# Head pairs in two halves of the array, or queries padded with zeros to all 128 rows

## The reference

```python
def forgetting_attention(q, k, v, log_f):          # A: 16 heads, causal, blocks of 128 queries
    c = jnp.cumsum(log_f, axis=1).transpose(0, 2, 1)
    for i in range(S // Q_BLOCK):
        s = einsum("bqhd,bkhd->bhqk", q[:, q0:q1], k[:, :q1]) * scale
        s = s + c[:, :, q0:q1, None] - c[:, :, None, :q1]
        p = softmax(where(causal, s, -inf))
        outs.append(einsum("bhqk,bkhd->bqhd", p, v[:, :q1]))

def dilated_branch(q, k, v, dil, slopes):          # B: 3 groups of 8 heads, dil = 1, 4, 16
    s = einsum("bnirhd,bnjrhd->bnrhij", qb, kk) * Dh ** -0.5
    s = where(valid, s - slopes * dil * dist, -inf)
    p = exp(s - max(s)); l = sum(p)                # o = (p / l) v, lse = max + log(l)
    # block: alpha = softmax of lse over the 3 groups, o = sum(alpha * o_g)
```

## Time and profile before

| | us |
|---|---|
| median of 3 runs (lowest, highest) | 2764.49 (2764.15, 2768.72) |
| profiled execution | 2764.49 |
| its span | 2762.7 |
| PE busy | 2673.2 (97%) |
| DVE busy | 1395.0 (50%) |
| ACT busy | 983.4 (36%) |
| POOL busy | 89.6 (3%) |

### The profile page before, as it was taken

One profiled execution on the slowest core, in us unless ns is written; L12 is line 12 of the kernel. 1 busy time (PEld: TensorE's weight loads), 2 busy tenths in 40 slices (PEclk: granted clock), 3 DMA queues, 4 the chain that ended last, 5 costly groups with the idle time before them and its releaser, 6 DMA issues.

```text
span 2762.7 us, 30936 instructions
## 1 busy us (share of the span) xinstructions
PE 2673.2 (97%) x12410; PEld 2151.1 (78%) x12410; DVE 1395.0 (50%) x2249; ACT 983.4 (36%) x1555; POOL 89.6 (3%) x99
## 2 busy tenths in 40 slices
PE   7999999999998699999998899999999999999999
PEld 6866888888787578888874588888888678888887
DVE  4455674664433667457557544434453155544342
ACT  3255442343225654234433432223312242422231
POOL 2000000000000000000010000000020220000000
PEclk9999999999999899999999899999999999999999
DMA  4300233233221022322321023322333022233222
GB/s 143 101 30 32 85 99 99 92 99 107 92 99 64 12 76 92 107 85 98 113 99 39 12 91 97 99 91 92 101 98 129 24 77 92 96 103 99 92 92 92
DMA packets 65520, 237.55 MB, mean 86 GB/s; under 512 B 7409, under 2 KB 7537, under 8 KB 65249
## 3 DMA queue, kind: packets, MB, share of 16 engines
q1 hardware_dynamic: 63648, 229.38, 25.6%
q0 software_dynamic: 1728, 6.19, 0.7%
HBM read 233.45 MB, written 2.10 MB: 85 GB/s over the span
## 4 chain that ended last, share of the span: by engine, by line
PE 90%; DVE 5%; ACT 4%; issue 1%; DMA 0%; SPq 0%; DVEq 0%; ACTq 0%
PE ps L420 28%; PE ps L422 28%; PE ps L421 28%; PE ps L525 2%; PE ps L799 1%; PE ps L561 1%; PE ps L542 1%; ACT m_A_P L1642 1%; ACT m_B_P L1642 1%; DVE m_B_P L948 1%; PE ps L786 1%; DVE m_A_st L952 1%; PE ps L497 0%; PE ps L483 0%; ACT m_E_P L1642 0%
## 5 line engine op out<-in xcount | busy, mean ns | idle before, releaser
L420 PE MATMUL ps<-m_xs,m_wsp 128*128 128x512 f32 x2232 | 880.6, 395 | 20.1 <-DVE m_xs L848 10.8
L422 PE MATMUL ps<-m_xs,m_wsp 128*128 128x512 f32 x2232 | 872.2, 391 | 0.0
L421 PE MATMUL ps<-m_xs,m_wsp 128*128 128x512 f32 x2232 | 871.8, 391 | 0.0
L1540 ACT ACTIVATE m_wsp<-m_raw 128x1024 fp32r<-128x1024 f32 x429 | 446.8, 1053 | 796.9 <-PE ps L422 761.9
L837 DVE TENSOR_TENSOR m_wsp<-m_raw,m_wsp 128x1024 fp32r<-128x1024 f32 x429 | 519.3, 1225 | 207.1 <-ACT m_wsp L1540 206.8
L420 PEld LDWEIGHTS ps<-m_xs,m_wsp 128*128 128x128 f32 x2232 | 421.5, 189 | 114.9 <-issue 18.4
L421 PEld LDWEIGHTS ps<-m_xs,m_wsp 128*128 128x128 f32 x2232 | 421.7, 189 | 89.3 <-issue 2.9
L422 PEld LDWEIGHTS ps<-m_xs,m_wsp 128*128 128x128 f32 x2232 | 421.0, 189 | 88.4
L887 DVE TENSOR_TENSOR m_x<-m_x,ps 128x512 f32<-128x512 f32 x104 | 70.8, 687 | 313.2 <-PE ps L422 313.2
L420 PE MATMUL ps<-m_wsp,m_xs 128*128 128x512 f32 x320 | 125.2, 391 | 0.0
L422 PE MATMUL ps<-m_wsp,m_xs 128*128 128x512 f32 x320 | 125.0, 391 | 0.0
(11 more groups left out here) (313 smaller groups left out, 3275.7 us busy)
## 6 DMA issues: line engine op xcount, KB each, us to landing
m_raw<-in_w SPq DMA_DIRECT2D x429, 512.0 KB, 3.3
m_x<-in_xT SPq DMA_DIRECT2D x4, 512.0 KB, 9.2
m_B_bias<-in_biasB POOLq DMA_DIRECT2D x8, 256.0 KB, 3.1
out<-m_x SPq DMA_DIRECT2D x8, 256.0 KB, 2.0
m_O_D<-in_decay POOLq DMA_DIRECT2D x1, 1024.0 KB, 5.1
m_A_sel<-in_sel POOLq DMA_DIRECT2D x1, 512.0 KB, 3.5
m_E_sel<-in_sel POOLq DMA_DIRECT2D x1, 512.0 KB, 3.5
m_O_cs<-in_ropeo POOLq DMA_DIRECT2D x1, 512.0 KB, 3.7
```

The lines of the kernel that those rows point to most:

```text
L420: e.matmul(out, lh, rh, start=first, stop=False)
L421: e.matmul(out, lh, rl, start=False, stop=False)
L422: return e.matmul(out, ll, rh, start=False, stop=final)
L1540: e.activation(wsp[n % NSP][:, 0, :], raw[n % NRAW][:, :], ACT.Copy).then_inc(*s_hi(n))
```

## The change

The queries of a head are copied by POOL into a tile of 128 partitions whose other half is zero (`A_qz`, two buffers for each parity; `B_qz`, one for each parity), with a new function `pad` and a new semaphore. A score matmul then multiplies this padded tile with all 128 partitions of `A_k` or `B_k`: the other head's keys meet zeros. Scores are issued job by job. `B_q` and `B_k` are stored in token order; in groups 1 and 2 the matmul itself reads every fourth column of both operands. In DVE's attention `among(i)` is moved ahead of `normalized(i-1)`. Two small tiles (`line`, `O_rc`) change place or size.

```diff
@@ tiles
-        line = sb(ctx, "line", [128, 24])
+        line = sb(ctx, "line", [128, 8])
+            A_qz = [ring(c, f"A_qz{p}", 2, [128, S]) for p in range(2)]
+                B_qz = [ring(c2, f"B_qz{p}", 1, [128, S]) for p in range(2)]
-            O_rc = sqs[1][:, 0:32].rearrange("p (h c) -> p h c", h=4)
+            O_rc = sb(c, "O_rc", [128, 4, 8])
@@ -511,27 +513,21 @@
                 P, PT = spec["P"], spec["PT"]
                 def scores(u):
-
                     for j in u.jobs:
                         b = take("score", pre, "score", j.n)
                         q.wait_ge(*free[b])
-                        free[b] = s_top[pre, j.n] if pre == "B" else s_exp[pre, j.n]
                         for w in spec["ready"](u, j):
                             q.wait_ge(*w)
-                    for si in range(len(u.jobs[0].segs)):
-                        last = {}
-                        for j in u.jobs:
-                            s = j.segs[si]
-                            last[j] = e.matmul(bank(pre, "score", j.n)[:, s["c0"]:s["c0"] + s["n"]], spec["q"](u, j, s),
-                                               spec["k"](u, j, s), start=True, stop=not spec["more"](j, s))
-                        for j in u.jobs:
-                            s = j.segs[si]
+                        for si, s in enumerate(j.segs):
+                            out = ps[b]
                             more = spec["more"](j, s)
+                            i = e.matmul(out[:, s["c0"]:s["c0"] + s["n"]], spec["q"](u, j, s), spec["k"](u, j, s),
+                                         start=True, stop=not more)
                             for ei, (o, n, lt, rh) in enumerate(more):
-                                last[j] = e.matmul(bank(pre, "score", j.n)[:, s["c0"] + o:s["c0"] + o + n], lt, rh,
-                                                   start=False, stop=ei == len(more) - 1)
-                            if s is j.segs[-1]:
-                                last[j].then_inc(*s_score((pre, j.n)))
+                                i = e.matmul(out[:, s["c0"] + o:s["c0"] + o + n], lt, rh, start=False,
+                                             stop=ei == len(more) - 1)
+                        i.then_inc(*s_score((pre, j.n)))
+                        free[b] = s_top[pre, j.n] if pre == "B" else s_exp[pre, j.n]
                 def turn(u):
                     for j in u.jobs:
@@ -586,13 +582,13 @@
             project_rows(ST["av"], xhalf, lambda k: s_xlo["mix0", k], lambda ci, tb: s_aev["av", ci, tb])
             def A_ready(u, j):
-                return [s_ev["ain", u.p], s_ev["ain", 8 + u.p], s_step["forget", "c"], d_sel["sel"], d_idb["idb"],
+                return [s_pad["A", u.p, j.par], s_ev["ain", 8 + u.p], s_step["forget", "c"], d_sel["sel"], d_idb["idb"],
                         d_mk["mk"], d_id["id"]]
             attention("A", A_units, dict(
                 P=A_P, PT=A_PT, before=nothing, among=nothing, ready=A_ready, vready=s_aev["av", 1, 3],
-                q=lambda u, j, s: A_q[64 * j.par:64 * j.par + 64, u.p, 128 * s["qb"]:128 * s["qb"] + 128],
-                k=lambda u, j, s: A_k[64 * j.par:64 * j.par + 64, u.p, 0:s["n"]],
+                q=lambda u, j, s: A_qz[j.par][u.p % 2][:, 128 * s["qb"]:128 * s["qb"] + 128],
+                k=lambda u, j, s: A_k[:, u.p, 0:s["n"]],
                 more=lambda j, s: [(s["n"] - 128, 128, identb[:, :], maskb[:, 0, :]),
                                    (0, s["n"], A_sel[:, j.h, :], A_c3[:, 0:s["n"]])],
                 v=lambda u, j, kb: A_v[:, kb, 64 * j.h:64 * j.h + 64],
@@ -624,6 +620,9 @@
             def B_tile(u):
                 return 4 * u.g + u.p
+            def B_tokens(u, s):
+                return slice(128 * s["qb"], 128 * s["qb"] + 128) if u.g == 0 else slice(s["qb"], S, 4)
             def B_stats(p, kind):
@@ -683,9 +682,10 @@
             attention("B", B_units, dict(
                 P=B_P, PT=B_PT, before=nothing, among=B_among, vready=s_aev["bv", 2, 3],
-                ready=lambda u, j: [s_ev["bq", B_tile(u)], s_ev["bk", B_tile(u)]],
-                q=lambda u, j, s: B_q[64 * j.par:64 * j.par + 64, B_tile(u), 128 * s["qb"]:128 * s["qb"] + 128],
-                k=lambda u, j, s: B_k[64 * j.par:64 * j.par + 64, B_tile(u), 128 * s["kbs"][0]:128 * s["kbs"][-1] + 128],
+                ready=lambda u, j: [s_pad["B", u.p, u.g, j.par], s_ev["bk", B_tile(u)]],
+                q=lambda u, j, s: B_qz[j.par][0][:, B_tokens(u, s)],
+                k=lambda u, j, s: B_k[:, B_tile(u), 128 * s["kbs"][0]:128 * s["kbs"][-1] + 128] if u.g == 0
+                else B_k[:, B_tile(u), s["qb"]:S:4],
                 more=lambda j, s: [],
                 v=lambda u, j, kb: B_v[:, kb, 512 * u.g + 64 * j.h:512 * u.g + 64 * j.h + 64],
                 evacuated=lambda u: s_ohi["B", B_tile(u)]))
@@ -983,9 +983,9 @@
                         spec["before"](units[i])
                         tops(units[i])
                         negated(units[i])
+                    spec["among"](i)
                     if 1 <= i <= n:
                         normalized(units[i - 1])
-                    spec["among"](i)
                     if i >= 3 and units[i - 3].final:
                         spec["out"](units[i - 3])
@@ -1151,18 +1151,12 @@
-            def by_fourth(m, t):
-                return t[:, :] if m < 4 else t[:, :].rearrange("p (i r) -> p r i", r=4)
...
-                    e.scalar_tensor_tensor(out=as_stored(m, B_q), in0=by_fourth(m, bank("bq", m)), scalar=0.125,
-                                           in1=by_fourth(m, rb("mix1")), op0=ALU.mult, op1=ALU.mult).then_inc(*s_ev(("bq", m)))
+                    e.scalar_tensor_tensor(out=B_q[:, m, :], in0=bank("bq", m)[:, :], scalar=0.125, in1=rb("mix1")[:, :],
+                                           op0=ALU.mult, op1=ALU.mult).then_inc(*s_ev(("bq", m)))
...
@@ -1978,6 +1970,22 @@
             e.memset(A_c3[:, :], 0.0)
             e.memset(A_onr[:, :], 1.0).then_inc(*s_zero("A"))
+            def pad(pre, key, par, dest, src, ready):
+                q.wait_ge(*ready)
+                own = slice(64 * par, 64 * par + 64)
+                e.tensor_copy(dest[own, :], src[own, :]).then_inc(*s_pad((pre, *key, par)))
+            q.wait_ge(*s_zero["A"])
+            for par in range(2):
+                for i in range(2):
+                    e.memset(A_qz[par][i][64 * (1 - par):64 * (1 - par) + 64, :], 0.0).then_inc(*s_zero(("A", par, i)))
+            for p in range(8):
+                for par in range(2):
+                    if p >= 2:
+                        q.wait_ge(*s_score["A", A_units[3 * (p - 2) + 2].jobs[-1].n])
+                    pad("A", (p,), par, A_qz[par][p % 2], A_q[:, p, :], s_ev["ain", p])
             def margins(n, after):
                 q.wait_ge(*after)
@@ -1988,18 +1996,27 @@
             margins(0, s_mm["aout", 7])
             q.wait_ge(*s_mm["f0.dn1", 7])
             e.memset(B_stat[:, :, :, :, :], 0.0).then_inc(*s_zero("B"))
+            q.wait_ge(*s_zero["B"])
+            for par in range(2):
+                e.memset(B_qz[par][0][64 * (1 - par):64 * (1 - par) + 64, :], 0.0).then_inc(*s_zero(("B", par)))
             for u in B_units:
                 if u.n == 4:
                     q.wait_ge(*s_mm["bv", 2, 3])
                     for half in range(2):
                         load(B_selp[half][:, :, :].bitcast(U16), a["selp"][:, 6 * half:6 * half + 6, :], d_selp[half], "selp")
+                    q.wait_ge(*s_pad["B", 0, 2, 1])
                     e.memset(B_pc[:, :, :], 0.0).then_inc(*s_zero("B2"))
                     q.wait_ge(*s_zero["B2"])
-                if u.first and u.g < 2:
-                    a0, a1 = (0, 256) if u.g == 0 else (256, 512)
-                    if u.p:
-                        q.wait_ge(*s_top["B", B_units[u.n - (3 if u.g == 0 else 2)].jobs[-1].n])
-                    load(B_bias[:, :, a0:a1], a["biasB"][:, 2 * u.p:2 * u.p + 2, a0:a1], d_bias[u.g], ("bias", u.p))
+                if u.first:
+                    for par in range(2):
+                        if u.n:
+                            q.wait_ge(*s_score["B", B_units[u.n - 1].jobs[-1].n])
+                        pad("B", (u.p, u.g), par, B_qz[par][0], B_q[:, 4 * u.g + u.p, :], s_ev["bq", 4 * u.g + u.p])
+                    if u.g < 2:
+                        a0, a1 = (0, 256) if u.g == 0 else (256, 512)
+                        if u.p:
+                            q.wait_ge(*s_top["B", B_units[u.n - (3 if u.g == 0 else 2)].jobs[-1].n])
+                        load(B_bias[:, :, a0:a1], a["biasB"][:, 2 * u.p:2 * u.p + 2, a0:a1], d_bias[u.g], ("bias", u.p))
             margins(1, s_mm["bout", 7])
             q.wait_ge(*s_mm["f1.dn1", 7])
             load(E_sel[:, :, :].bitcast(U16), a["sel"], d_selE, "sel")
```

8 lines of the change are left out of this document (2 added, 6 removed).

## The result

The kernel after takes 2786.16 us (median of 4 runs, 2782.41 to 2789.69), the kernel before 2765.34 beside it: a ratio of 1.0074, 95% interval 1.0055 to 1.0091. It is slower by 20.8 us, where 17.2 were forecast (9.2 in A and 8 in B), and the time lies inside the range. The working behind the number did not hold: one term was far too large, and a cause that had been set to zero carries most of the loss.

The account below looks back on a forecast made before the run. TensorE was taken to bound stage A, and a loop of scores, DVE's maxima and ACT's exponentials stage B. 2764.49 + 9.2 (A) + 8 (B) = 2782 us, range 2768 to 2802.

Parts of the forecast that it names:

- Scores in A: Stage A: padded heads run one after the other, costing TensorE more; +9.2 us, between +7.5 and +11.0.
- Stride in B: Stage B, groups 1 and 2: slow strided weight loads set 0.23 us a pass, 3.7 us a unit.
- first rival: Stage B scores: load and stream slowed in turn, 0.46 us a pass, +30 us, 2812 us; chance 0.15.
- the second (free): Rival, stage B scores: the stride costs nothing, B -4 us, 2770 us in sum; chance 0.25.
- B as a whole: Stage B: 5.3 us over three pair periods and 2.5 for the first, +8 us, between -4 and +38.
- +2.5 us for the first pair: Stage B, first pair: copies and strided scores come in a row, +2.5 us once, from 0 to 5.
- the order's -0.8: Stage B, DVE: mixing ahead of the normalization reaches TensorE's transposes 0.8 us earlier, once a pair.
- the zero for group 0: Stage B, group 0: contiguous scores, first head's maxima beside the second's scores; zero, give or take 0.3 us.
- POOL's copies: Two padding copies take 2.1 us, hidden in A and covered in B, the bias load behind them with little room.
- Evacuations of B without the stride: Before stage B: query and key evacuations lose their stride, zero gain since the projection hides them.
- The two moved tiles issue nothing: Tiles `line` and `O_rc`: they issue no instructions, and no cost was counted for moving them.
- third rival: Stage B: strides free and TensorE's clock above 0.95, 10.6 us shorter, 2757 us; chance 0.05.

Follow-up runs that it names:

- jobwise: Kernel before with the scores of A, B and E issued head by head, queries still in halves, no padding; 2784.88 us, ratio 1.0058.
- kcontig: Kernel after with `line` at 24 columns, `O_rc` back in scratch, B's k for groups 1 and 2 stored by fourths, q still strided; 2771.36 us, ratio 1.0023 to before.
- qcontig: Kernel after with `line` at 24 columns, `O_rc` back in scratch, B's q for groups 1 and 2 stored by fourths, k still strided; 2770.33 us, ratio 1.0021 to before.
- contig: Kernel after with `line` at 24 columns, `O_rc` back in scratch, B's q and k stored by fourths and read contiguously; 2767.47 us, ratio 1.0001 to before.
- wgap: Kernel before with weights `wsp` moved 128 bytes, `line` at 16 columns, activation tiles moved 256, 128, 512 and 384 bytes; 2817.48 us, ratio 1.0185.
- ejob: Kernel before with the scores of stage E alone issued head by head; 2762.29 us, ratio 0.9986.
- fact64: Kernel before with a 64-byte gap ahead of the activation tile in each of the four feed-forward blocks; 2773.63 us, ratio 1.0028.

## Why the prediction was right in its number and wrong in its working

**Scores in A: +9.2 us forecast, +0.1 to +1.4 measured.** This step failed, by its own criterion (a pair under 11.6 us). The new price of the groups was right, to 0.1 us. What failed is the sentence that the end of the stage gets all that TensorE gets. One pair of before, timeline of TensorE: the pieces between the scores.

```profile
202.05 0.88 PE L542 MATMUL ps<-m_ident,m_A_P 128*128 128x128 f32 x6
...
204.71 1.16 PE L561 MATMUL ps<-m_A_PT,m_A_v 128*64 128x128 f32 x12
205.80 0.88 PE L542 MATMUL ps<-m_ident,m_A_P 128*128 128x128 f32 x6
...
208.22 1.25 PE L561 MATMUL ps<-m_A_PT,m_A_v 128*64 128x128 f32 x12 [0.16 <-ACT m_A_PT L1651]
209.41 1.09 PE L542 MATMUL ps<-m_ident,m_A_P 128*128 128x128 f32 x8
```

and of after:

```profile
224.11 0.88 PE L538 MATMUL ps<-m_ident,m_A_P 128*128 128x128 f32 x6
224.82 0.39 PE L524 MATMUL ps<-m_A_k,m_A_qz 128*128 128x128 f32 x2
...
226.89 0.88 PE L557 MATMUL ps<-m_A_PT,m_A_v 128*64 128x128 f32 x12
227.69 0.88 PE L538 MATMUL ps<-m_ident,m_A_P 128*128 128x128 f32 x6
...
230.23 0.97 PE L557 MATMUL ps<-m_A_PT,m_A_v 128*64 128x128 f32 x12
231.13 1.09 PE L538 MATMUL ps<-m_ident,m_A_P 128*128 128x128 f32 x8
```

The scores of before that the first mark leaves out start at 202.86. From start to next start, in a pair: the scores of the three units with their bf16 matmuls grow from 1.85 + 1.62 + 1.71 = 5.18 us to 2.07 + 1.82 + 2.35 = 6.24, +1.06 (the float32 groups +1.48, the bf16 ones -0.42, where I had +1.38 and -0.22; 0.16 us of the latter was TensorE's wait for ACT at 208.22, which stood in the scores' share). The two products with V of 12 matmuls shrink from 1.09 and 1.19 to 0.80 and 0.90 us, -0.58, and the transposes ahead of the scores by 0.09 each, -0.27. In sum +0.21, and the pair measured +0.22. The V products of before held a wait that TensorE's busy share hid, since it lay for the greater part with the weight loads; before, then after:

```profile
PEld ps L561 <- ACT m_A_PT L1651: 5.6, 17, 0.5
```

```profile
PEld ps L557 <- ACT m_A_PT L1643: 1.5, 4, 0.5
```

jobwise, which has the new order with the old 64 rows, tells two causes apart. Its V products of 12 matmuls take 0.81 us (226.79 in its chain), about what the padded ones take (0.80 and 0.90), and its weight loads wait for ACT for the same 1.5 us in 4 places, so this part is not the padding's. The heads' scores now come one after the other, so that DVE and ACT start on the first while TensorE is at the second; but the scores also take longer in both kernels, which gives ACT time as well. Which of these took the wait away no run shows. The transposes are another matter: ahead of jobwise's 64-row groups they keep the length of before (0.81 us at 227.60), so they shrank because the group behind them now has 128 rows. The Trainium skill, TensorEngine Tiling (Array Packing), Key Properties, says that a change of tiling mode drains TensorE; I had counted that only inside the rows of the scores, while 0.09 us of each change stood in the rows ahead of them. The stage as a whole took 94.3 to 94.5 us in the five padded kernels and 92.9 to 94.2 in the eight with A unchanged: +0.1 by the two profiles of before and after, +1.4 by the medians (94.4 and 93.0), which is near 8 x 0.21.

**Stride in B: right in its price, for half the reason.** I took 0.23 us a pass and 3.7 us a unit; measured 0.24 and 3.87. I argued from the slow weight load with the stream free beside it. The load is slow, as the earlier trace rows showed, and kcontig shows that it sets this pace alone; but qcontig shows that the stream is as slow by itself. The first rival (load and stream in turn, 0.46) is excluded, and so is the second (free). The Trainium skill, SBUF — State Buffer, Door 1: The DMA port swizzle, has an access to a new 16-byte line pay each time; the runs agree that either operand pays, and show that the two payments overlap. The chain's pair became 2.6 us longer where I had 1.75.

**B as a whole: +8 forecast, +12.4 by the two profiles, +10.0 against the median of seven B's.** Of it contig gives the stride about 6 (115.1 to 109.3, at a clock of 0.91 and 0.86). The rest is 3.8 us over that median, more than six of the seven unchanged profiles show and less than the seventh (111.2). The +2.5 us for the first pair, the order's -0.8 and the zero for group 0 can't be told apart in it. That the mixing now follows the negation at once was seen (919.77, then 920.50), without a gain in time.

**POOL's copies.** Two of them mostly last 1.2 us, not 2.1 (median 0.61 each; the longest one in A took 1.54 us and the longest in B 1.50): 64 partitions cost less than the 32-partition copy of the earlier trace rows, which was no good neighbour. They are hidden in A (no wait of TensorE for POOL). In B the "little room" of 0.7 us was used up: the bias load came last on the chain at 938.41. The working's sign was a wait of at most 1 us each time; it was 3.6 us in two, the longer one 1.9.

**Evacuations of B without the stride: zero.** The stretch from F0 to B took 203.4 us in both kernels that dropped both strides, 203.9 to 207.1 in eleven others that keep at least one (wgap, whose weights are moved, apart). Most of the 2.3 us to before is the clock's: the stretch ran at a granted clock of 0.99 before and 1.00 after, and jobwise, ejob and fact64, with both strides and a clock of 1.00, took 203.9 to 204.2. That leaves at most 0.8 us for the evacuations.

**E was not in the working at all.** The loop in `scores` is shared, so E changed too. It gained: -2.2 us by the two profiles, -4.6 against the median of the seven with the old order, and 0.05 to 0.23% of the kernel when done alone.

**"The two moved tiles issue nothing."** True and beside the point, since they move the tiles behind them, and those TensorE reads. This sentence is where the prediction failed most: +15.4 us, in the F blocks and O_go. No rival had it, since all of them looked for instructions that change.

So 2782 came out near 2786 by luck. By the two profiles the working had 9.1 us too much in A and left out the 2.2 and 2.3 us gained in E and ahead of B; against that it had 4.4 too little in B and never counted 15.4. Taken against the medians of the kernels whose stage is unchanged, A is +1.4, B +10.0, E -4.6, the stretch ahead of B -2.3 and blocks and O_go +15.4, in sum 19.9 of the 20.8 us. The third rival (B's clock above 0.95) did not occur: 0.88.

## What to carry to other kernels

Read a diff for what it does to addresses and not only to instructions: here an unread tile that shrank by 64 bytes cost 17 us alone and 15 of the change's 20.8, and the sign of it is a matmul duration that moves in stages which nobody touched. A TensorE that is busy for 98% of a head pair's time may still hold waits inside its groups; compare each group from start to next start with the same group elsewhere, and look at the waits of the weight loads, before added work is priced in full. Ask of a shared loop which other stages it serves, and try its parts stage by stage: one of them (E) was a gain. And before a slow stretch is put down to one operand, count what else runs in it: half of each block's matmuls read another tile.

## What the runs showed of the hardware that was not expected

- Matmuls of 128x512 fp32r in a row: 528 of them keep TensorE busy for 120.0 us when moving operand and weights begin at the same place within 256 bytes (both at 128 or both at 0), for 123.0 to 123.5 us when they don't (+2.5 to +2.9%), and for 121.2 with the weights at 128 and the moving operand at 192.
- float32 passes of 128 columns with a 16-byte stride: 0.24 us whether the weights, the stream or both are strided (3.79, 3.89 and 3.87 us for 16), 0.12 with neither (1.95).
- A 64-row score group between 128-row work costs 0.19 us more than the padded 128-row one, at 128 and at 512 columns, and about 0.09 more in the group ahead of it (0.81 against 0.72 us for six transposes).
- POOL copied 64 partitions by 512 float32 in 0.61 us (median of 40), while 32 partitions took 1.03 from another source.
- Stage B with the same code took 103.1 to 111.2 us in seven profiles, at granted clocks from 0.77 to 0.87, and E with the old order 63.3 to 67.1: a difference of a few us in such a stage between two single profiles shows nothing.
